# Weight loads from the fifth piece on move from SyncE's queue to GpSimd's, placing transfers from three engines to two

## What is computed

```python
h = rmsnorm(x, norm_g)
(qa, ka, va, ga, qb, kb, vb, ab, gb, cq, ckv, kr, gc, mg) = split_cols(h @ w_in)
ya = swa_sink_attention(qa, ka, va, a_sinks) * silu(ga);   za = ya @ w_oa
yb = rmsnorm(gla_chunk_readout(qb, kb, vb, log_a)) * silu(gb);   zb = yb @ w_ob
yc = mla_attention(q_nope, q_rope, k_nope, k_rope, v_c) * silu(gc);   zc = yc @ w_oc
y = m[:, :, 0] * za + m[:, :, 1] * zb + m[:, :, 2] * zc
return x + y @ w_out
```

## Time and profile before

| | us |
|---|---|
| median of 3 runs | 926.05 (925.83 to 926.31) |
| the profiled execution, its own time | 926.16 |
| its span, first to last instruction | 924.4 |
| TensorE (PE) busy | 916.8, 99% |
| VectorE (DVE) busy | 609.8, 66% |
| ScalarE (ACT) busy | 390.1, 42% |
| GpSimd (POOL) busy | 31.7, 3% |

### The profile page before, as it was taken

One profiled execution on the slowest core, in us unless ns is written; L12 is line 12 of the kernel. 1 busy time (PEld: TensorE's weight loads), 2 busy tenths in 40 slices (PEclk: granted clock), 3 DMA queues, 4 the chain that ended last, 5 costly groups with the idle time before them and its releaser, 6 DMA issues.

```text
span 924.4 us, 13093 instructions
## 1 busy us (share of the span) xinstructions
PE 916.8 (99%) x5092; PEld 752.6 (81%) x5092; DVE 609.8 (66%) x1006; ACT 390.1 (42%) x728; POOL 31.7 (3%) x68
## 2 busy tenths in 40 slices
PE   9999999999999999999999999999999999999997
PEld 7988888888888777888889888888888887778886
DVE  7976468448567877575459655674567668876834
ACT  7453335224543454432444433442363425553324
POOL 0000000000000001000000000000000000100000
PEclk9999999999999999999999999999999999999999
DMA  8424325232534345422233423253235333444542
GB/s 294 126 93 137 114 69 159 91 102 83 154 113 134 90 137 161 137 90 92 92 115 94 125 92 112 62 169 96 88 114 160 103 115 115 133 143 137 150 124 91
DMA packets 42909, 110.98 MB, mean 120 GB/s; under 512 B 8608, under 2 KB 11552, under 8 KB 42720
## 3 DMA queue, kind: packets, MB, share of 16 engines
q1 hardware_dynamic: 36736, 100.62, 34.2%
q10 hardware_dynamic: 4064, 5.33, 2.1%
q0 software_dynamic: 2048, 4.20, 1.6%
HBM read 85.41 MB, written 2.23 MB: 95 GB/s over the span
## 4 chain that ended last, share of the span: by engine, by line
PE 94%; DVE 2%; ACT 2%; DMA 1%; SPq 1%; issue 0%; DVEq 0%; ACTq 0%
PE ring L671 72%; PE nat L671 9%; PE nat L879 3%; PE aux L902 2%; PE nat L858 1%; PE nat L686 1%; PE nat L685 1%; PE nat L687 1%; DMA raw<-pieces 1%; PE ring L686 1%; PE ring L685 1%; PE ring L687 1%; PE nat L749 1%; DVE merged L1227 1%; DVE w_lo L1249 1%; ACT work L1146 1%
## 5 line engine op out<-in xcount | busy, mean ns | idle before, releaser
L671 PE MATMUL ring<-act_hi,w_hi 128*128 128x512 f32 x784 | 307.9, 393 | 0.0
L671 PE MATMUL ring<-act_lo,w_hi 128*128 128x512 f32 x784 | 305.4, 390 | 0.0
L671 PE MATMUL ring<-act_hi,w_lo 128*128 128x512 f32 x784 | 305.1, 389 | 0.0
L919 ACT ACTIVATE w_hi<-raw 128x1024 fp32r<-128x1024 f32 x152 | 161.7, 1064 | 334.2 <-PE ring L671 260.5
L1249 DVE TENSOR_TENSOR w_lo<-raw,w_hi 128x1024 fp32r<-128x1024 f32 x152 | 184.6, 1216 | 97.8 <-ACT w_hi L919 97.6
L671 PEld LDWEIGHTS ring<-act_hi,w_hi 128*128 128x128 f32 x784 | 147.1, 188 | 38.0 <-issue 8.1
L671 PEld LDWEIGHTS ring<-act_hi,w_lo 128*128 128x128 f32 x784 | 147.2, 188 | 31.0
L671 PEld LDWEIGHTS ring<-act_lo,w_hi 128*128 128x128 f32 x784 | 147.2, 188 | 29.7
L1600 DVE SCALAR_TENSOR_TENSOR gates<-ring,rstd 128x512 f32<-128x512 f32 x72 | 49.3, 685 | 78.4 <-PE ring L671 78.3
L671 PE MATMUL ring<-y_hi,w_hi 128*128 128x512 f32 x192 | 74.9, 390 | 0.0
L671 PE MATMUL ring<-y_hi,w_lo 128*128 128x512 f32 x192 | 74.7, 389 | 0.0
(11 more groups left out here) (237 smaller groups left out, 1037.7 us busy)
## 6 DMA issues: line engine op xcount, KB each, us to landing
raw<-pieces SPq DMA_DIRECT2D x152, 512.0 KB, 3.5
bank_g<-work SPq DMA_DIRECT2D x80, 64.0 KB, 2.7
lat<-work SPq DMA_DIRECT2D x48, 64.0 KB, 2.8
bank_g<-work POOLq DMA_DIRECT2D x40, 64.0 KB, 2.5
bank_g<-work ACTq DMA_DIRECT2D x40, 64.0 KB, 3.2
xt<-x_t SPq DMA_DIRECT2D x8, 256.0 KB, 5.2
bank_a<-work SPq DMA_DIRECT2D x32, 64.0 KB, 2.0
bank_g<-bank_a SPq DMA_DIRECT2D x16, 128.0 KB, 3.9
```

The lines of the kernel that those rows point to most:

```text
L671: mm = pe.matmul(dst, stationary, moving, start=start and i == 0, stop=stop and i == 2)
L919: nc.scalar.activation(w_hi[:, n % HL, :], raw[:, n % RAW, :], ACT.Copy).then_inc(hi_split.sem, 1)
```

## The change

SyncE's load of the loop goes away; GpSimd's placing goes away, and it gets a loop that only waits for the slot and loads. ScalarE's wait before the high split takes a new semaphore for these pieces. SyncE issues parts 0 to 11 of each placement, ScalarE parts 12 to 15.

```diff
-TURN_PARTS, SP_PARTS, ACT_PARTS = 16, 8, 12
+TURN_PARTS, SP_PARTS = 16, 12
...
+        raw_next = [sig(f"raw_next{i}", 0) for i in range(RAW)]
...
-                sp.wait_ge(lo_split.sem, n - RAW + 1)
-                sp.dma_start(raw[:, n % RAW, :], pieces[n]).then_inc(raw_loaded[n % RAW].sem, 16)
...
-                        pe.wait_ge(turned_placed.sem, turned_placed.at(layer, 16 * ACT_PARTS * (3 + i)))
-                        pe.wait_ge(turned_placed_pool.sem, turned_placed_pool.at(layer, 16 * POOL_PARTS * (3 + i)))
+                        pe.wait_ge(turned_placed.sem, turned_placed.at(layer, 16 * TURN_PARTS * (3 + i)))
...
-                act.wait_ge(raw_loaded[n % RAW].sem, 16 * (n // RAW + 1))
+                if n <= RAW:
+                    act.wait_ge(raw_loaded[n % RAW].sem, 16 * (n // RAW + 1))
+                else:
+                    act.wait_ge(raw_next[n % RAW].sem, 16 * (n // RAW - (n % RAW == 0)))
...
-                        for n in range(SP_PARTS, ACT_PARTS):
+                        for n in range(SP_PARTS, TURN_PARTS):
                             place_blocks(act, i, n, turned_placed)
...
-            for layer in range(DEPTH):
-                pool.wait_ge(head_blocks.sem, head_blocks.at(layer, 4))
-                pool.wait_ge(read_done.sem, read_done.at(layer, 4))
-                for n_part in range(ACT_PARTS, TURN_PARTS):
-                    place_blocks(pool, 0, n_part, head_placed_pool)
-                for group in range(2 + n_sets):
-                    pool.wait_ge(blocks_set.sem, blocks_set.at(layer, 4 * group + 4))
...
-                    for n_part in range(ACT_PARTS, TURN_PARTS):
-                        place_blocks(pool, group, n_part, turned_placed_pool)
+            for n in range(RAW + 1, DEPTH * PIECES):
+                pool.wait_ge(lo_split.sem, n - RAW + 1)
+                pool.dma_start(raw[:, n % RAW, :], pieces[n]).then_inc(raw_next[n % RAW].sem, 16)
```

More of the change, by code:

```diff
@@ L471, in build_hybrid_trunk @@
         neg_top_set, exp_done = sig("neg_top_set", TT + 2 * n_sets), sig("exp_done", n_steps)
[L472 to L475, removed]
+        blocks_set, turned_placed = sig("blocks_set", n_steps), sig("turned_placed", 16 * TURN_PARTS * (2 + n_sets))
+        value_done, head_placed = sig("value_done", TT + n_sets), sig("head_placed", 16 * TURN_PARTS)
         denom_set, divided = sig("denom_set", 2 * TT * A_KV + 2 * n_sets), sig("divided", TT * A_KV + 2 * n_sets)
@@ L885, in _ @@
                         pe.wait_ge(exp_done.sem, exp_done.at(layer, NA))
-                        pe.wait_ge(turned_placed.sem, turned_placed.at(layer, 32 * ACT_PARTS))
-                        pe.wait_ge(turned_placed_pool.sem, turned_placed_pool.at(layer, 32 * POOL_PARTS))
+                        pe.wait_ge(turned_placed.sem, turned_placed.at(layer, 32 * TURN_PARTS))
                         for t in range(TT):
@@ L1475, in _ @@
                         if i == 0:
-                            dve.wait_ge(head_placed.sem, head_placed.at(layer, 16 * ACT_PARTS))
-                            dve.wait_ge(head_placed_pool.sem, head_placed_pool.at(layer, 16 * POOL_PARTS))
+                            dve.wait_ge(head_placed.sem, head_placed.at(layer, 16 * TURN_PARTS))
                             dve.wait_ge(silu_set.sem, silu_set.at(layer, BR))
@@ L1556, in _ @@
                         if group == 0:
-                            dve.wait_ge(head_placed.sem, head_placed.at(layer, 16 * ACT_PARTS))
-                            dve.wait_ge(head_placed_pool.sem, head_placed_pool.at(layer, 16 * POOL_PARTS))
-                        else:
-                            dve.wait_ge(turned_placed.sem, turned_placed.at(layer, 16 * ACT_PARTS * group))
-                            dve.wait_ge(turned_placed_pool.sem, turned_placed_pool.at(layer, 16 * POOL_PARTS * group))
+                            dve.wait_ge(head_placed.sem, head_placed.at(layer, 16 * TURN_PARTS))
+                        else:
+                            dve.wait_ge(turned_placed.sem, turned_placed.at(layer, 16 * TURN_PARTS * group))
                         for k in (range(2 * (i % 2), 2 * (i % 2) + 2) if name == "turn_a" else range(4)):
```

## The result

The changed kernel takes 938.26 us (937.02 to 938.48, 4 runs) against 925.94 for the kernel before (925.60 to 926.31, 4 runs): ratio 1.013, interval 1.0118 to 1.0141. Forecast were 926.1 and a range up to 928.1. The profiled execution has a span of 936.5 us, 12.1 more than before.

The account below looks back on a forecast made before the run. TensorE was taken to bound the kernel, busy 916.8 of 924.4 us. Start 6.3 + middle 912.3 + end 5.8, nothing added, plus 1.76 outside the span is 926.16, median 0.11 below; forecast 926.1, range 925.2 to 928.1.

Parts of the forecast that it names:

- the two stretches outside the middle: TensorE's first 6.3 us and the last 5.8 us after its last matmul; nothing added or removed in either.
- the loads' own cover: Weight loads arrive ten microseconds before their split needs them; landing 0.4 us later, at most 3.9, costs TensorE nothing.
- The fifth piece: First load moved to GpSimd: issued at 12.1, latest landing that TensorE does not feel 26.5, margin 6.7 us.
- Rival A: GpSimd writes descriptors only while VectorE idles: TensorE stalls 3.3 to 6.7 us once, at the fifth piece; 931; chance 0.08.
- The rule that I weighed: GpSimd issues need the port shared with VectorE; each held for at most one fast-mode copy or tensor_scalar, sum unchanged.
- The heads' placement: VectorE's wait at 150.82 grows from 0.60 to 3.1 to 4.5 us, twice; hidden from TensorE, 2.9 us to spare.
- SyncE places 12 parts instead of 8: Turned sets' placements: last part 2.54 us later; thinnest margin of 14 is 4.6 us, left 2.0; no cost.
- a load beside a part: Loads now run beside placing parts: 1.4 us more landing time put on the parts, 0.6 us margin still left.
- gain on TensorE 0: Loads leaving SyncE start up to 4.96 us earlier at 16 placing groups, but arrive early anyway, so TensorE gains nothing.
- can only come earlier: SyncE's rotated queries and last rows, no longer behind a load's wait, are never later than before; no size given.
- Rival B: Placement too late: SyncE issues at twice 0.634 us, perhaps two groups a layer, 937; half that contention, 929; chance 0.05.

Follow-up runs that it names:

- the run with one load: The kernel before with the changed 12/4 placing split and only the 49th piece's load of each layer on GpSimd, the others on SyncE: 931.20 us, ratio 1.0052.
- the run with held loads: The changed kernel, GpSimd waiting before the 48th piece's load of each layer until the second turned set is placed in full: 929.37 us, ratio 1.0040.
- the run with two loads on GpSimd: The changed placing split, only the 48th and 49th piece's loads of each layer on GpSimd, the other 146 on SyncE: 935.98 us, ratio 1.0104.

## Why the prediction was wrong

What bounds the kernel, the two stretches outside the middle, and what I said of the loads' own cover held. GpSimd issues a load in 527 ns (I took 500), and it lands in 3.7 us, where SyncE's took 3.5. The fifth piece was issued at 12.3 and took 6.5 us, 18.8 against a due time of 26.5:

```profile
L1201 POOL DMA_DIRECT2D raw<-pieces x150: 527/527/664, 12.3 to 900.9; - x150
...
DMA to landing us min/median/max: 3.6/3.7/7.2
```

Rival A, starved descriptors, did not happen. The rule that I weighed (the Trainium skill, SBUF — State Buffer, "SBUF: two separate sides") holds a GpSimd issue while such a VectorE instruction runs, which with the longest of L1551 allowed half a microsecond each. This trace shows a little of that kind: of the 150 issues five took over 0.55 us, the fifth piece's (664 ns) and four of 0.58 to 0.61 us, and those four are the ones that began while VectorE ran the tensor_scalar of L1538 (L1551 before). Whether it is that hold no run isolates; under 0.1 us, four times, plays no part in the loss.

The heads' placement held too. VectorE's wait went from 0.60 to 4.4 us, near the upper end of the 3.1 to 4.5 that I had, and TensorE felt nothing.

The step that failed is "SyncE places 12 parts instead of 8". I wrote that the thinnest of the 14 placements of turned sets has a margin of 4.6 us. It has 1.4: the second turned set, landed at 255.5 and read by TensorE at 256.9. The figure of 4.6 is right for the set that I showed in the earlier trace rows, but I had looked for the next reader in VectorE, which for most sets comes first. The second set is the last of branch A: the next turning starts at 314.64, 59 us after it has landed, and its reader is `values_a`. Nor is 4.96 us the longest group of eight on SyncE, as I wrote; the one of this very set took 5.41. The delay that I had worked out, 2.54 us, passes the margins of 1.4 and 1.6 us by 1.1 and 0.9, and the run with the placing split alone measures that: waits of 1.6 and 0.8.

A second term was mis-sized. For a load beside a part I took 1.4 us, from the load's own lengthening; in the changed kernel the last parts land 3.3 and 2.7 us later, and with one load ahead 2.3. In each of these cases a part of 64 KB went out behind a load of 512 KB that was still under way. I had read the queue only as something that held loads back ("gain on TensorE 0"), and not as what kept them behind the parts; in the same way I wrote that SyncE's other transfers "can only come earlier", and not what they would then run beside. The Trainium skill (DMA: Bandwidth & Descriptors, "Issuing engines are not separate DMA queues") says that transfers share the same DMA engines whoever issues them; the traces agree: the parts' landing went from 2.0 to 5.3 us while these engines were 0.84 busy.

The third part of the loss, 3 us by the slower clock behind the waits, stood nowhere in my working. Rival B had the right side and the right kind of place, with a margin three times too wide, and 0.05 of the chance. That its 937 is near the measured 938.26 is luck: it has every issue twice as long and two groups a layer late, but one group a layer was late, most issues stayed at 0.59 us, and half of the lateness came from the landing. Its sum is off besides: from the first of twelve parts to the last there are 11 steps, so that at the doubled step the last is 9.5 us later, not 10.1.

## What to carry to other kernels

A shared queue is also an order: before a bulk transfer moves to a queue of its own, list the small urgent transfers that it stood behind, and hold the bulk one until they have landed, where it has the time to spare. A margin is found by going through every reader of every instance, engine by engine, and taking the least; a row that shows a comfortable one says nothing of the others. An engine that is idle in sum can still be the wrong one to issue from, when its issues come ahead of the work that the bound engine waits for.

## What the runs showed of the hardware

The drop of the clock is not a plain matter of how long TensorE waits. After waits of 5.52, 3.81 and 2.21 us the values ran at 0.69 to 0.70. After one of 3.46 us (one load on GpSimd) they ran at 1.00, and so they did after 1.63, 0.95, 0.80 and 0.74:

```profile
260.50:264.30 3.80, 3.79 (x65) 3.63 (x66) 2.53 (x4) 0.63 (x1) 0.00 (x0) 1.00 0.02 5
```

```profile
259.48:264.90 5.42, 5.42 (x65) 5.25 (x66) 3.12 (x4) 1.22 (x2) 1.58 (x3) 0.69 0.75 254
```

The first row is the run with one load, after 3.46 us; the second the run with held loads, after 2.21 us. Nor does the drop have to be there when TensorE starts again: in the run with two loads on GpSimd, after the 2.79 us of the second layer, the first 16 matmuls still took 1.09 us, as in the kernel before, and the 48 behind them 4.49 instead of 2.79. The "about 2 us" of the expectation for one load is thus not borne out. What decides stays open. SyncE's and ScalarE's issues of 0.5 to 0.6 us were at times stretched near 250 us into the run, on both engines at once: in the changed kernel to 2.11 us on SyncE (from 250.4) and 1.84 on ScalarE (from 250.7), both ending at 252.5. In the kernel before they took 1.04 and 1.40 there, both ending at 252.2. What holds them was not tried.
